# Gate projection of the odd mixer: 512 + 256 columns, the halves added on VectorE, the multiply on GpSimd

## The reference

```python
def odd_mixer(h, w_in, out_norm, w_out, pos):
    ...
    z = h @ w_in
    q = rope(z[..., :nq] ...)
    k = rope(z[..., nq:2 * nq] ...)
    v = z[..., 2 * nq:2 * nq + nv] ...
    g = z[..., 2 * nq + nv:]
    o = rmsnorm(retention(q, k, v), out_norm)
    o = o.reshape(B, S, nv).astype(h.dtype) * jax.nn.silu(g)
    return o @ w_out
```

## Time and profile before

| | |
|---|---|
| median of three runs | 2344.2 us |
| the profiled execution's own time | 2344.32 us |
| its span, first to last instruction | 2342.5 us |
| instructions | 37935 |
| TensorE busy | 2322.1 us (99%) |
| VectorE busy | 1763.8 us (75%) |
| ScalarE busy | 1276.7 us (55%) |
| GpSimd busy | 79.8 us (3%) |
| mean granted clock of TensorE | 0.999 |

### The profile page before, as it was taken

The page is one execution under the profiler, slowest core; times in us unless marked ns, Lnnn a source line. Parts: engine busy times, 40 slices in busy tenths (PEclk is TensorE's granted clock), DMA queues, the critical chain, the costliest instruction groups (busy, mean ns, idle before and its releaser), DMA issues.

```text
span 2342.5 us, 37935 instructions
## 1 busy us (share of the span) xinstructions
PE 2322.1 (99%) x15336; PEld 2120.1 (91%) x15336; DVE 1763.8 (75%) x2652; ACT 1276.7 (55%) x1993; POOL 79.8 (3%) x96
## 2 busy tenths in 40 slices
PE   8999999999999999999999999999999999999998
PEld 7988889998888888999999888998889999998887
DVE  6889657779758876887569886688767875698854
ACT  6855454655445544675555554455445855565542
POOL 0012000002100000020000000000000200000000
PEclk9999999999999999999999999999999999999999
DMA  6455565446556555654355555556555533456563
GB/s 227 136 185 193 188 207 166 145 158 210 177 183 208 189 187 186 200 163 125 118 172 181 189 189 182 169 194 202 188 189 190 175 119 120 160 171 223 188 184 107
DMA packets 115454, 412.48 MB, mean 176 GB/s; under 512 B 12880, under 2 KB 14800, under 8 KB 115024
## 3 DMA queue, kind: packets, MB, share of 16 engines
q1 hardware_dynamic: 114992, 407.96, 53.3%
q0 software_dynamic: 288, 2.10, 0.3%
HBM read 408.96 MB, written 1.05 MB: 175 GB/s over the span
## 4 chain that ended last, share of the span: by engine, by line
PE 90%; DVE 7%; ACT 1%; POOL 1%; issue 1%; DMA 0%; SPq 0%; DVEq 0%; POOLq 0%; ACTq 0%
PE ps L423 89%; DVE wlo L1891 2%; DVE region L2605 1%; ACT region L1375 0%; PE ps L698 0%; ACT whi L1175 0%; POOL region L2991 0%; POOL region L2992 0%; DMA raw<-in_ew_c 0%; DVE xx L2113 0%; DVE region L2160 0%; DVE RX L2077 0%; DVE x L2106 0%; DVE x L1943 0%; DVE region L2163 0%
## 5 line engine op out<-in xcount | busy, mean ns | idle before, releaser
L423 PE MATMUL ps<-xx,whi 128*128 128x256 f32 (+1 forms) x4920 | 1239.0, 341 | 2.0 <-DVE xx L1951 0.9
L1891 DVE TENSOR_TENSOR wlo<-raw,whi 128x1024 fp32r<-128x1024 f32 (+3 forms) x772 | 927.6, 1208 | 292.0 <-ACT whi L1175 290.8
L1175 ACT ACTIVATE whi<-raw 128x1024 fp32r<-128x1024 f32 (+3 forms) x772 | 801.7, 1044 | 581.2 <-PE ps L423 540.7
L423 PE MATMUL ps<-xx,wlo 128*128 128x256 f32 x3696 | 833.2, 280 | 0.0
L423 PEld LDWEIGHTS ps<-xx,wlo 128*128 128x128 f32 x3696 | 699.2, 189 | 109.5
L423 PEld LDWEIGHTS ps<-xx,whi 128*128 128x128 f32 x4920 | 764.7, 190 | 7.4 <-issue 3.4
L423 PE MATMUL ps<-H,whi 128*128 128x512 f32 (+1 forms) x2144 | 546.6, 343 | 1.3 <-DVE wlo L1891 1.3
L423 PE MATMUL ps<-H,wlo 128*128 128x256 f32 x1632 | 364.8, 279 | 0.0
L423 PEld LDWEIGHTS ps<-H,wlo 128*128 128x128 f32 x1632 | 308.5, 189 | 49.8
L423 PEld LDWEIGHTS ps<-H,whi 128*128 128x128 f32 x2144 | 333.2, 190 | 2.5 <-issue 2.0
L1886 DVE TENSOR_REDUCE t<-ps 128x256 f32<-128x512 f32 x308 | 211.6, 689 | 46.0 <-PE ps L423 39.4
(11 more groups left out here) (293 smaller groups left out, 1556.9 us busy)
## 6 DMA issues: line engine op xcount, KB each, us to landing
raw<-in_sg SPq DMA_DIRECT2D x128, 512.0 KB, 4.1
raw<-in_su SPq DMA_DIRECT2D x128, 512.0 KB, 4.2
raw<-in_sd SPq DMA_DIRECT2D x128, 512.0 KB, 4.3
raw<-in_mw_g SPq DMA_DIRECT2D x48, 512.0 KB, 3.5
raw<-in_fg SPq DMA_DIRECT2D x44, 512.0 KB, 3.3
raw<-in_fu SPq DMA_DIRECT2D x44, 512.0 KB, 3.2
raw<-in_fd SPq DMA_DIRECT2D x32, 512.0 KB, 3.6
raw<-in_mw_a SPq DMA_DIRECT2D x24, 512.0 KB, 4.2
```

What stands on the lines that cost most here:

```text
L423: return e.matmul(out, lhsT, rhs, start=start, stop=stop, skip_group_check=True)
L1175: e.activation(m.whi[:, c % NHL, 0:cw], m.raw[:, c % NRAW, 0:cw], ACT.Copy).then_inc(s["whi"].h, s["whi"].up(c))
L1891: e.tensor_tensor(m.wlo[:, c % NHL, 0:cw], m.raw[:, c % NRAW, 0:cw], m.whi[:, c % NHL, 0:cw].bitcast(F32), ALU.subtract).then_inc(s["wlo"] ...
```

## The change

The sixteen gate chunks are issued by `gemm_wide`. VectorE adds the two halves of the bank into `sg` with `both`, in the place of the multiply. The multiply with `R` goes to GpSimd as a new function `gates`, in place on `sg`, between the `R` multiplies of the two SwiGLUs in its program. ScalarE's Silu waits for GpSimd's signal in place of VectorE's. Nothing is moved in an engine's order, and no transfer is added.

```diff
@@ tensor_program, odd
-            gemm_fm("ow_g", i, take(i % 4, ("rdve", "g", i))[:, 0:256], xh, xl)
+            gemm_wide("ow_g", i, take(i % 4, ("rdve", "g", i)))
@@ scalar_program, odd
-            w.wait_ge(s["rdve"], "g", i)
+            w.wait_ge(s["rpool"], i)
             e.activation(m.sg[:, i, :], m.sg[:, i, :], ACT.Silu).then_inc(s["ract"].h, s["ract"].up("g", i))
@@ vector_program, odd
             w.wait_ge(s["gemm"], "ow_g", i)
-            e.tensor_tensor(m.sg[:, i, :], ps[i % 4][:, 0:256], R[:, 0, :], ALU.mult).then_inc(
-                s["rdve"].h, s["rdve"].up("g", i))
+            both(m.sg[:, i, :], ps[i % 4]).then_inc(s["rdve"].h, s["rdve"].up("g", i))
@@ gpsimd_program
+    def gates():
+        w.wait_ge(s["rstd"], "o")
+        for i in range(16):
+            g = m.sg[:, i, :]
+            w.wait_ge(s["rdve"], "g", i)
+            e.tensor_tensor(g, g, m.R[:, 0, :], ALU.mult).then_inc(s["rpool"].h, s["rpool"].up(i))
...
     norm("f0", 22)
+    gates()
     norm("f1", 22)
```

More of the change, by code:

```diff
@@ L382 @@
     "rdve",
+    "rpool",
     "pact",
```

## The result

The changed kernel takes 2349.32 us (median of 15 runs, 2347.65 to 2350.55) against 2344.2 us (median of 15, 2344.05 to 2344.53): 5.1 us more, a ratio of 1.0022 with a 95% interval of 1.0015 to 1.0029. The runs of the changed kernel lie in three bunches: two near 2347.8, ten near 2349.3, three near 2350.4. Those of before lie within 0.5 us. The profiled execution is of the middle bunch, 2349.26 us with a span of 2347.5, 5.0 above the span of before.

What follows compares the result with a forecast made beforehand. The prediction took TensorE's issue as the bound of the gate stage. Its terms, -1.54 + 2.1 + 0.2 + 4.2 + 0.1 = +5.1 us on 2344.2, gave 2349.3 us, with an 8-in-10 range of 2343.6 to 2352.6.

Steps and rivals of the forecast that it cites:

- Gain of TensorE: Gate stage: wide matmuls save a third instruction per k, 0.096 us a chunk, 1.54 us over sixteen chunks.
- Path from evacuation to Silu: Reduction, hand-over and GpSimd's multiply delay Silu: 2.49 us after its evacuation beside a cast, 1.55 for Silu 7.
- VectorE held up at the port: GpSimd's multiply blocks a two-input VectorE instruction next in line, taken as 0.61 us, bounded by 0 and 0.61.
- Root of head 0: First tour, ScalarE: root ready at 411.04, so the reciprocal starts 1.33 us after evacuation 5 where it was 0.34.
- The backlog at evacuation 4: VectorE, behind the blocked cast before evacuation 4: delays Silu 4 by 0.24 us.
- First wait: TensorE, before head 1's products: waits 2.1 us for VectorE's decay pair, done at 424.02.
- Sum of head 1: Second tour: TensorE's sum for head 1 waits 0.2 us for the addition behind ScalarE's late copies and squares.
- Second wait: TensorE at bank 3, output chunk 0's last quarter: waits 4.2 us for evacuation 15, 3.3 plus 0.9 from a later root.
- Behind the last wait: After bank 3: 0.1 us for restarting the matmul pipeline; all engines follow TensorE again from output chunk 4.
- The first rival: Cover holds: VectorE isn't blocked, multiplies take 0.75 us; waits 1.0 and 2.2, sum +1.6, 2345.8 us; chance 0.13.
- the second: Pure gain: decay pair not on TensorE's path, everything hidden, 1.54 us gain left, 2342.7 us; chance 0.09.
- the third: Port loss everywhere: VectorE's chains pass GpSimd over or weight casts slip 0.6 a chunk; 2351.7 us and up; chance 0.10.

## Why the prediction was right

The time was predicted at 2349.3 us and measured at 2349.32. The mechanism was right: evacuation to GpSimd to Silu to the heads' work, and from there to the decay pair and to bank 3. That the number fits to 0.02 is luck. The waits came out 1.7 us smaller than predicted, and a fall of the clock that was no term of the sum gave 1.6 back. In the two lowest executions of fifteen, near 2347.8, the sum was too high by 1.5. The mark that the prediction set for slower, 2348.9, is a ratio of 1.0020 and lies inside the measured interval (1.0015 to 1.0029): that the change is slower is shown, that it is past this mark is not.

- **Gain of TensorE:** 1.54 predicted, 1.35 measured. The steps of the heads in between cost the same in both: from head 1's scores to the next gate matmul it is 416.29 - 415.06 = 1.23 us here and 417.11 - 415.88 = 1.23 before. It is the k that was mis-sized: between neighbouring gate chunks of this stage it takes 0.359 to 0.360 us narrow and 0.349 wide, 0.0104 apart on average, where the rows from other stages gave 0.012.
- **Path from evacuation to Silu:** the mechanism was right. Beside a cast the multiply took 1.55 us (406.80 to 408.35, with a cast until 407.85), so 0.50 after it; with VectorE idle it took 0.64, where 0.75 was taken. Silu 7 followed evacuation 7 by 421.14 - 419.70 = 1.44, predicted 1.55.
- **VectorE held up at the port:** taken as 0.61 with no row to show it. It is real and smaller: the gating multiply at 416.38 took 0.75 in place of 0.43, and a cast at 404.45 took 1.66 in place of 1.22, both with a multiply of GpSimd's in progress. That it is GpSimd's doing, the halves of the change show: the same gating multiply took 0.75 (at 416.42) where GpSimd multiplied and nothing was added, and 0.43 (at 417.04) where VectorE added and multiplied and GpSimd did nothing. The Trainium skill's rule ("SBUF — State Buffer", "Who interferes with whom") that these two kinds exclude each other agrees with these rows in both directions. That the later one stands still for the whole of the other can't be read from them: the two overlap for 0.46 us (416.38 to 416.84), and the gating multiply grew by 0.32.
- **Root of head 0:** reciprocal predicted 1.33 after evacuation 5, measured 410.62 - 409.69 = 0.93. The backlog at evacuation 4 (0.24) did not come, and Silu 4 followed its evacuation by 2.34, not 2.49.
- **First wait:** decay pair predicted at 424.02, measured 422.91 + 0.28 = 423.19; wait predicted 2.1, measured 1.30. The 0.8 are the earlier root (0.4), the smaller loss at the port (0.3) and Silu 7 (0.1).
- **Sum of head 1:** 0.2 predicted, none. The addition ended at 431.28, 0.29 before TensorE's sum at 431.57.
- **Second wait:** 4.2 predicted, all at bank 3; 3.5 measured, of which 0.59 idle already at bank 2. The release came 0.8 sooner than predicted: evacuation 15 ended 450.43 - 435.43 = 15.0 after evacuation 12 began, where 14.88 and the extra 0.9 for the root made 15.8. The extra itself was right, 0.91 (1.84 against 0.93); what was too high is what the second tour took over from the first.
- **Behind the last wait:** the sum had 0.1 us here, for the restart, and nothing for the clock. The restart itself was 0.10; the clock fell to 1.2 GHz behind bank 3 and cost 1.58 more. This is the term that was missing.

So the waits together were 6.5 predicted and 4.8 measured, and restart and clock 0.1 and 1.7. The first rival (cover holds, 2345.8), the second (pure gain, 2342.7) and the third (port loss at every chunk) did not come; the pure gain came when ScalarE's order and one cast were changed.

## What to carry to other kernels

A handful of nanoseconds per instruction on the busiest engine is worth only what the slack of its narrowest waits lets through. Before lengthening a helper's latency, list what stands in order behind each wait of the engine that consumes it: here the Silu was in no hurry, but the heads' work queued behind it was. The cure is order: put the urgent work ahead of the wait for a slow helper, and move a cast that has time out of the stretch in which VectorE has no gap.

## What the hardware showed that was not expected

- After a wait of 2.4 us, with one of 0.59 just before it, the granted clock fell from full to half (0.50 from 450.60 to 451.90, full again from 453.90), and the distance of the matmuls went from 0.12 to 0.21. With one wait of 2.87 us it fell in one profile and stayed at full in two. With waits of about 2.1 to 2.2 us the times still fall in two bunches, about 1.6 us apart, which a fall in some executions would explain; only lower ones were profiled. With 1.3 us (2345.54 to 2346.30), 1.4 us (one run of ten at 2347.18) and 0.9 us (2343.75 to 2343.87) they hardly do. A wait of TensorE can cost 1.7 times its length (2.42 and 1.68 behind it), and makes the time less steady.
- GpSimd's multiply of 128 x 256 takes 0.64 us alone, 0.81 to 1.02 beside a short VectorE instruction with two SBUF inputs and 1.55 beside a cast. A VectorE instruction with two SBUF inputs that starts while it runs grows by 0.3 to 0.45 us (0.43 to 0.75, 1.22 to 1.66).
